# Merge-gate blocks placed between the column groups of an input projection, on one Trainium2 core

## The reference

```
xn = rmsnorm(h, norm_mix)
z = xn @ w_in
y_a = nsa_mixer(...) @ w_branch_nsa
y_b = dsa_mixer(...) @ w_branch_dsa
gate = sigmoid(g_merge)
h = h + (gate[..., :D] * y_a + gate[..., D:] * y_b) @ w_out
h = h + (silu(hn @ w_gate) * (hn @ w_up)) @ w_down
```

## Time and profile before

| | us |
|---|---|
| median of 3 runs | 1840.47 (1840.46 to 1841.13) |
| profiled execution, its own time | 1840.48 |
| span of the profiled execution | 1838.8 |
| TensorE busy in the span | 1707.3 (93%) |
| VectorE busy | 1208.7 (66%) |
| ScalarE busy | 701.4 (38%) |
| GpSimd busy | 567.1 (31%) |
| TensorE's share of the chain that ended last | 78% |

### The profile page before, as it was taken

One profiled execution on the slowest core, in us unless ns is written; L12 is line 12 of the kernel. 1 busy time (PEld: TensorE's weight loads), 2 busy tenths in 40 slices (PEclk: granted clock), 3 DMA queues, 4 the chain that ended last, 5 costly groups with the idle time before them and its releaser, 6 DMA issues.

```text
span 1838.8 us, 25573 instructions
## 1 busy us (share of the span) xinstructions
PE 1707.3 (93%) x9248; PEld 1467.2 (80%) x9248; DVE 1208.7 (66%) x2181; ACT 701.4 (38%) x1398; POOL 567.1 (31%) x396
## 2 busy tenths in 40 slices
PE   6789989999999999999999999899999999889994
PEld 5667778888898989889988877688888888668883
DVE  6689778999243545566646516667676676458976
ACT  5543433311274457655532114422322222234443
POOL 3303232322040012322212121544454445245451
PEclk9899989999999989999999999999999999989997
DMA  5103232532242001001015523122333222853432
GB/s 178 46 12 105 71 102 73 174 92 91 50 136 115 13 24 47 12 13 35 1 44 163 169 90 120 50 94 87 123 117 104 86 87 75 297 200 98 156 102 92
DMA packets 152590, 172.21 MB, mean 94 GB/s; under 512 B 18961, under 2 KB 102929, under 8 KB 152209
## 3 DMA queue, kind: packets, MB, share of 16 engines
q1 hardware_dynamic: 152464, 170.57, 28.9%
HBM read 121.00 MB, written 49.55 MB: 93 GB/s over the span
## 4 chain that ended last, share of the span: by engine, by line
PE 78%; DVE 10%; ACT 3%; DMA 3%; issue 3%; POOL 1%; SPq 1%; DVEq 0%; ACTq 0%; POOLq 0%
PE psA L1335 13%; PE psA L1336 13%; PE psA L1337 13%; PE psT L1517 9%; PE psT L1342 7%; PE psT L1336 5%; PE psT L1337 5%; PE psT L1335 5%; PE psA L1402 3%; PE psA L1401 3%; DMA act_raw<-scratch_act 1%; DVE rotated L1776 1%; DVE equal L1836 1%; POOL w_lo L377 1%; DVE above L1836 1%
## 5 line engine op out<-in xcount | busy, mean ns | idle before, releaser
L377 POOL TENSOR_TENSOR w_lo<-w_raw,w_hi 128x1024 fp32r<-128x1024 f32 (+2 forms) x52 | 119.9, 2314 | 243.3 <-ACT w_hi L372 243.3
L1188 ACT ACTIVATE p<-s,nmax 128x640 f32<-128x640 f32 (+7 forms) x192 | 143.9, 750 | 121.4 <-DVE nmax L1949 120.8
L995 POOL TENSOR_TENSOR w_lo<-w_sum,w_hi 128x1024 fp32r<-128x1024 f32 x44 | 115.5, 2626 | 129.4 <-ACT w_hi L1243 129.4
L1342 PE MATMUL psT<-ident,p 128*128 128x128 f32 x816 | 131.2, 282 | 19.2 <-DVE yTl_dsa L2008 4.7
L1018 POOL TENSOR_TENSOR w_lo<-act_raw,w_hi 128x512 fp32r<-128x512 f32 x77 | 104.9, 1366 | 137.8 <-ACT w_hi L1272 137.8
L2161 DVE TENSOR_TENSOR w_lo<-wd,w_hi 128x512 fp32r<-128x512 f32 x77 | 96.5, 1257 | 66.9 <-ACT w_hi L1279 66.6
L1335 PE MATMUL psA<-w_hi,xTh 128*128 128x512 f32 (+2 forms) x320 | 124.5, 389 | 13.6 <-POOL w_lo L377 9.5
L1336 PE MATMUL psA<-w_lo,xTh 128*128 128x512 f32 (+2 forms) x320 | 120.4, 376 | 0.0
L1337 PE MATMUL psA<-w_hi,xTl 128*128 128x512 f32 (+2 forms) x320 | 120.1, 375 | 0.0
L1342 PEld LDWEIGHTS psT<-ident,p 128*128 128x128 f32 x816 | 98.8, 154 | 26.4 <-ACT p L1188 7.0
L372 ACT CAST w_hi<-w_raw 128x1024 fp32r<-128x1024 f32 (+2 forms) x52 | 52.3, 1014 | 151.0 <-PE psA L1337 108.9
(11 more groups left out here) (351 smaller groups left out, 4949.1 us busy)
## 6 DMA issues: line engine op xcount, KB each, us to landing
act_raw<-scratch_act SPq DMA_DIRECT2D x77, 256.0 KB, 2.6
w_raw<-in_w_in_dram SPq DMA_DIRECT2D x28, 512.0 KB, 3.8
scratch_act<-act SPq DMA_DIRECT2D x33, 256.0 KB, 2.1
scratch_act<-act_sum SPq DMA_DIRECT2D x33, 256.0 KB, 2.1
scratch_gates<-gate_out SPq DMA_DIRECT2D x32, 256.0 KB, 3.1
gates<-scratch_gates SPq DMA_DIRECT2D x32, 256.0 KB, 4.1
wd<-in_w_down_dram SPq DMA_DIRECT2D x4, 1536.0 KB, 7.7
a<-in_w_gate_dram SPq DMA_DIRECT2D x22, 256.0 KB, 3.2
```

Source lines behind the costliest of these rows:

```text
L377: nc.gpsimd.tensor_tensor(self.lo[n % RING][:, 0:u], self.raw[n % RAW][:, 0:u], self.hi[n % RING][:, 0:u].bitcast(F32), ALU.subtract).then ...
L995: nc.gpsimd.tensor_tensor(lo2[n % RING][:], block_of(n)[:], hi2[n % RING][:].bitcast(F32), ALU.subtract)\
L1188: a_.activation(p_sb[v % PR][:, 0:n], s_sb[v % 2][:, 0:n], ACT.Exp, scale=-1.0, bias=nmax[:, BR[a], i, h:h + 1], accum_out=psum_p[:, BR[a] ...
L1342: mm = pe.transpose(bank[:, P * n:P * (n + 1)], src, ident[:])
```

## The change

The steps get one common list, `main`: after QB, CMP and WKV three gate blocks (six steps) each, after QA the other seven (14 steps). The list of weight pieces follows the same order. Slots, PSUM banks, loads, stores, spills, splits and turns go by positions in this list. A piece is due as before, at the step that frees its slot. ScalarE and GpSimd handle the first due piece ahead of their work on the step and the others behind it, which on ScalarE is behind `z_evac` but ahead of `block_hi` and `turned_out` of the steps before. VectorE does two passes of the bisection in each projection step and five in each gate step. Some hunks are left out: the release conditions of the ring slots and the bank number of an evacuation, rewritten for the new positions, and ScalarE's old gate loop.

```diff
--- before.py
+++ after.py
@@ -279,9 +279,18 @@
     def chunk_items(src, first, width):
         return [[(src[:, 2 * n:2 * n + 2, first:first + width], 0, 2, width)] for n in range(KT // 2)]

-    items1 = sum((chunk_items(w_in, *COLS[c]) for c in ORDER), [])
-    NCH = len(items1)
-    items1 += [[(w_in[:, :, o_gm + P * j:o_gm + P * (j + 1)], 0, KT, P)] for j in range(2 * KT)]
+    GATES_AFTER = {IDX: 0, QB: 3, CMP: 3, WKV: 3, QA: 7}
+    items1, main, chunk_at, gate_at = [], [], {}, []
+    for ch, c in enumerate(ORDER):
+        chunk_at[ch] = len(items1)
+        items1 += chunk_items(w_in, *COLS[c])
+        main += [("z", NT * ch + i) for i in range(NT)]
+        for _ in range(GATES_AFTER[c]):
+            j = len(gate_at)
+            gate_at.append(len(items1))
+            items1.append([(w_in[:, :, o_gm + P * j:o_gm + P * (j + 1)], 0, KT, P)])
+            main += [("g", 2 * j), ("g", 2 * j + 1)]
+    pos_of = {step: n for n, step in enumerate(main)}
     wa = A["w_branch_nsa"][0].rearrange("(k p) c -> p k c", p=P)
     wb = A["w_branch_dsa"][0].rearrange("(k p) c -> p k c", p=P)
     wo = A["w_out"][0].rearrange("(k p) c -> p k c", p=P)
@@ -332,7 +341,11 @@
     tg = {k: n for n, k in enumerate(tgroups)}

     Z_STEPS, G_STEPS = 8 * len(ORDER), 4 * KT
-    free1 = [8 * (n // 4) + 7 if n < NCH else Z_STEPS + 2 * (n - NCH) + 1 for n in range(len(items1))]
+    free1 = [0] * len(items1)
+    for ch, n in chunk_at.items():
+        free1[n:n + 4] = [pos_of["z", NT * ch + NT - 1]] * 4
+    for j, n in enumerate(gate_at):
+        free1[n] = pos_of["g", 2 * j + 1]
     M_STEPS, O_STEPS, F_STEPS = 2 * KT, 2 * NT, FT
     free2 = [2 * j + 1 for j in range(KT)] + [M_STEPS + 8 * (n // 4) + 7 for n in range(8)]

...
@@ -645,12 +657,6 @@
                 dst, src = kD["slc" if c == CMP else "win"][:, :, tok(i)], t[:, 0:4, :]
             sp.dma_start(dst, src.bitcast(F32)).then_inc(spilled[n % 2], 16)

-        for q in range(Z_STEPS + 3):
-            if q < Z_STEPS:
-                for n in w1.due(q, RAW + RING):
-                    w1.load(sp, n)
-            if q >= 3:
-                spill(q - 3)
         def load_q(k):
             set_, i = ("dsa", k) if k < NT else ("nsa", k - NT)
             if k >= 2:
@@ -665,15 +671,19 @@
             load_q(0)
             load_q(1)

-        for g in range(G_STEPS):
-            for n in w1.due(Z_STEPS + g, RAW + RING):
-                w1.load(sp, n)
-            if g == 4:
+        last_z = pos_of["z", Z_STEPS - 1]
+        for at_, (kind, n) in enumerate(main):
+            for item in w1.due(at_, RAW + RING):
+                w1.load(sp, item)
+            if kind == "g":
+                sp.wait_ge(g_out, n + 1)
+                sp.dma_start(gD[n // 2, :, HALF * (n % 2):HALF * (n % 2 + 1)], gst[n % 2][:])\
+                    .then_inc(g_stored[n % 2], 16)
+            if at_ >= 3 and main[at_ - 3][0] == "z":
+                spill(main[at_ - 3][1])
+            if at_ == last_z + 5:
                 sp.wait_ge(zt_ps, len(turned))
                 first_queries()
-            sp.wait_ge(g_out, g + 1)
-            sp.dma_start(gD[g // 2, :, HALF * (g % 2):HALF * (g % 2 + 1)], gst[g % 2][:])\
-                .then_inc(g_stored[g % 2], 16)


         sp.wait_ge(g_ps, G_STEPS)
@@ -897,13 +907,14 @@

         for n in range(RING):
             w1.split_lo(pool, n)
-        for q in range(Z_STEPS):
-            for n in w1.due(q, RING):
-                w1.split_lo(pool, n)
-            rope_cos(q)
-        for g in range(G_STEPS):
-            for n in w1.due(Z_STEPS + g, RING):
-                w1.split_lo(pool, n)
+        for at_, (kind, n) in enumerate(main):
+            due = w1.due(at_, RING)
+            for item in due[:1]:
+                w1.split_lo(pool, item)
+            if kind == "z":
+                rope_cos(n)
+            for item in due[1:]:
+                w1.split_lo(pool, item)

         pool.wait_ge(g_ps, G_STEPS)
         pool.wait_ge(pos_in, 16 * 4)
...
@@ -1097,16 +1108,26 @@
                     last = a_.copy(tq[s_ % 2][:, 4 * g:4 * g + 4, :], ps)
                 last.then_inc(zt_out, 1)

-        def stage2(first, stop):
-            for q in range(first, stop + 2):
-                if q < stop:
-                    for n in w1.due(q, RING):
-                        w1.split_hi(act, n)
-                    z_evac(q)
-                if first <= q - 1 < stop:
-                    block_hi(q - 1)
-                if first <= q - 2 < stop:
-                    turned_out(q - 2)
+        def gate_evac(g):
+
+            act.wait_ge(g_ps, g + 1)
+            if g >= 2:
+                act.wait_ge(g_stored[g % 2], 16 * (g // 2))
+            a_.activation(gst[g % 2][:], psA[:, pos_of["g", g] % 4, :], ACT.Sigmoid).then_inc(g_out, 1)
+
+        def stage2():
+            for at_ in range(NT, len(main)):
+                due = w1.due(at_, RING)
+                for n in due[:1]:
+                    w1.split_hi(act, n)
+                kind, n = main[at_]
+                (z_evac if kind == "z" else gate_evac)(n)
+                for n in due[1:]:
+                    w1.split_hi(act, n)
+                if main[at_ - 1][0] == "z" and at_ > NT:
+                    block_hi(main[at_ - 1][1])
+                if main[at_ - 2][0] == "z" and at_ > NT + 1:
+                    turned_out(main[at_ - 2][1])

         def id_relu(v):

@@ -1130,9 +1151,12 @@
                 for n in range(2, RING):
                     w1.split_hi(act, n)
             if 0 <= k - 1 < NT:
-                for n in w1.due(k - 1, RING):
+                due = w1.due(k - 1, RING)
+                for n in due[:1]:
                     w1.split_hi(act, n)
                 z_evac(k - 1)
+                for n in due[1:]:
+                    w1.split_hi(act, n)
             if 0 <= k - 2 < NT:
                 block_hi(k - 2)
             if 0 <= k - 3 < NT:
...
@@ -1358,21 +1375,26 @@
                 turn4(turn_bank(("x", i, g)), [xs[i % 2][:, P * k:P * (k + 1)] for k in range(4 * g, 4 * g + 4)])\
                     .then_inc(xt_ps, 1)

+        def bank_out(at_):
+
+            kind, n = main[at_]
+            return (z_out if kind == "z" else g_out), n + 1
+
         def z_step(q):
             c, i = zsteps[q]
             width = COLS[c][1]
-            if q >= 4:
-                pe.wait_ge(z_out, q - 3)
+            if pos_of["z", q] >= 4:
+                pe.wait_ge(*bank_out(pos_of["z", q] - 4))
             if q == NT:
                 pe.wait_ge(sc_done, len(iunits))
             if q < NT:
                 pe.wait_ge(xl_done, 2 * (q + 1))
             for a in range(KT // 2):
-                n = 4 * (q // NT) + a
+                n = chunk_at[q // NT] + a
                 if i == 0:
                     pe.wait_ge(w1.lo_done, n + 1)
                 hi, lo = w1.parts(n, 2)
-                mm = three(psA[:, q % 4, 0:width],
+                mm = three(psA[:, pos_of["z", q] % 4, 0:width],
                            [((xTh[:, 2 * a + k, tok(i)], xTl[:, 2 * a + k, tok(i)]), (hi[:, k, :], lo[:, k, :]))
                             for k in range(2)], a == 0, a == KT // 2 - 1)
                 if i == NT - 1 and a < KT // 2 - 1:
@@ -1388,12 +1410,20 @@
                     src = [kcvc[q % 2][:, P * b:P * (b + 1)] for b in range(2)]
                 turn4(turn_bank(("z", q, g)), src).then_inc(zt_ps, 1)

-        def stage2(first, stop):
-            for q in range(first, stop + 2):
-                if q < stop:
-                    z_step(q)
-                if first <= q - 2 < stop - 3:
-                    z_turn(q - 2)
+        def gate_step(g):
+            n, half = gate_at[g // 2], slice(HALF * (g % 2), HALF * (g % 2 + 1))
+            pe.wait_ge(w1.lo_done, n + 1)
+            pe.wait_ge(*bank_out(pos_of["g", g] - 4))
+            hi, lo = w1.parts(n, KT)
+            three(psA[:, pos_of["g", g] % 4, :], [((hi[:, k, :], lo[:, k, :]), (xTh[:, k, half], xTl[:, k, half]))
+                                                  for k in range(KT)]).then_inc(g_ps, 1)
+
+        def stage2():
+            for at_ in range(NT, len(main)):
+                kind, n = main[at_]
+                (z_step if kind == "z" else gate_step)(n)
+                if main[at_ - 2][0] == "z" and at_ > NT + 1:
+                    z_turn(main[at_ - 2][1])

         def scores(ps, q_, k_hi, k_lo, n):

@@ -1427,19 +1457,7 @@
                 id_unit(v)
         for v in range(EARLY, len(iunits)):
             id_unit(v)
-        stage2(NT, Z_STEPS)
-        for g in range(G_STEPS):
-            if g in (1, 2, 3):
-                z_turn(Z_STEPS - 4 + g)
-            n, half = NCH + g // 2, slice(HALF * (g % 2), HALF * (g % 2 + 1))
-            pe.wait_ge(w1.lo_done, n + 1)
-            if g < 4:
-                pe.wait_ge(z_out, Z_STEPS - 3 + g)
-            else:
-                pe.wait_ge(g_out, g - 3)
-            hi, lo = w1.parts(n, KT)
```

(50 more changed lines are left out.)

22 lines of the change are left out of this document (7 added, 15 removed).

## The result

Over 20 executions of each, the changed kernel takes **1846.31 us** (1843.22 to 1849.75) and the kernel before 1841.62 (1838.85 to 1845.89): ratio **1.0022, 95% interval 1.0015 to 1.0029**, slower by 4.1 us (2.8 to 5.3). The forecast was 1848.3 in a range of 1837 to 1855, with a chance of 0.70 for slower: the right side, with the time 2.0 us too high and the difference, +7.9 us, nearly twice the measured one. The profiled execution took 1847.43 us (span 1845.7).

What follows compares the result with a forecast made beforehand. TensorE was taken to set the time. Losses of 1.5 (slow start), 24.2 (entries), 9.6 (clock), 1.5 (exits) and 0.5 (VectorE's end) make 37.3 us against 29.4 before: +7.9 on 1840.48, so 1848.3 us, range 1837 to 1855.

Steps and rivals of the forecast that it cites:

- The mechanism: At group ends, block_hi queues on ScalarE behind three pieces, so block_lo is late; TensorE idles 6.5 us after QB's gate step.
- The entries: TensorE's stalls going from projection groups into gate blocks: 6.5 us at QB and QA, 4.3 CMP, 6.9 WKV; 24.2 together.
- The port: At the entries, GpSimd's running low half was taken to hold VectorE's block_lo; if not, 8.6 us less.
- rival A: block_lo isn't held by GpSimd's low half: 8.6 us less, 1839.7 us, no change; chance 0.13.
- The clock: TensorE at half clock after the four entry stalls, mean 2.4 us lost each: 9.6 us, bounds 7.4 and 12.
- Exits and tail: Gate blocks to the next group: 0.5 us each for three exits, 1.5 us; VectorE's end after QA: 0.5 us.
- so VectorE is through 75.6 us after it: After QA's released block_lo, VectorE's 32 passes (33.4 us) and selection (39.4 us), starting about 2.7 us behind it.
- the 353.1 needed: Time the five stretches from QB to the gates would need with turns counted where they stand: 353.1 us together.
- the slow start: Loss of about 1.5 us in the stretch that lies outside the change, counted among losses before and after.
- Passes and order at nothing: Single bisection passes on VectorE and the new order of splits: each costed at 0; order's bounds -1 and +1 us.
- IDX's end: First group's end under the new split order: evacuation earlier, block_hi a little later, scores start as now; 0 us.
- Rival B: Entries are hidden as intended, the fourth piece's cast ending by about 10.5: 24.5 us less, 1816 us; chance 0.09.

Runs made afterwards that it cites:

- experiment 1: Changed kernel, but after the first group ScalarE does block_hi and turned_out ahead of the second to fourth weight piece: 1823.85 us, ratio 0.9902.
- experiment 6: Changed kernel with block_hi and turned_out ahead of the second to fourth piece in all groups, the first too: 1820.64 us, ratio 0.9877.
- experiment 10: Kernel of experiment 6, with the fourth piece cast after the next gate step's evacuation and block_hi, and three passes per CMP step: 1822.63 us, ratio 0.9882.
- experiment 11: Kernel of experiment 6 unchanged, run again beside experiment 12 on one chip: 1823.15 us, ratio 0.9884 to the kernel before.
- experiment 12: Kernel of experiment 10 unchanged, run again beside experiment 11 on one chip: 1815.38 us, ratio 0.9846 to the kernel before.
- experiment 5: Kernel before, with single bisection passes alone: two per projection step behind IDX, the rest in the gate steps: 1840.24 us, ratio 0.9991.
- experiment 4: Kernel before, with the new order of splits alone (one piece ahead of the evacuation, others behind) on ScalarE and GpSimd: 1849.86 us, ratio 1.0037.
- experiment 7: Changed kernel, with bisection passes saved up until six are due and then made as a whole bit: 1854.79 us, ratio 1.0066.
- experiment 8: Changed kernel, with all due pieces split ahead of the evacuation on ScalarE and of rope_cos on GpSimd: 1849.42 us, ratio 1.0026.

## Why the prediction was right, and where its terms were off

**The mechanism** held as written, shown by experiment 1. Counted from the start of QB's last step (157.54), the forecast had the second low half from 7.8 to 10.2, the fourth cast from 14.0 to 15.0, block_hi done at 15.6, block_lo held to 17.5 and done at 18.2. Measured were 7.7 to 10.3, 14.2 to 15.2, 15.7, and TensorE going on at 18.2. The gate step ended at 12.0 and not 11.8.

**The size** is partly luck. The difference was forecast at +7.9 us and measured at +4.1 (2.8 to 5.3). The time itself came within 2.0 us because the forecast was added to one execution of the kernel before, 1840.48, where 20 have a median of 1841.62. In the profiled pair the stretch grew by 5.1 us where 7.4 were forecast.

**The entries** were 0.3, 0.6, 1.5 and 0.3 us shorter than forecast: 21.5 against 24.2. The largest error is WKV's: the first low half ended 4.6 us after the step's start and not 4.9, and was needed at 3.75 and not 3.5 (the cost there 0.94 and not 1.4); the wait for blocks behind it was 4.5 and not 5.5, which no single row explains.

**The port** was the doubtful term, taken from another instruction's rows. After has block_lo's own row, 2.34 us. The Trainium skill (SBUF — State Buffer, Who interferes with whom) has this rule, and the trace agrees: it picked the right one of two readings. Freed, the four waits lost 6.0 us; rival A priced it at 8.6. What a held block_lo loses is 2.34 less 0.68, 1.7 us, not the 2.4 of a whole low half; the forecast's own times (free to begin at 15.6, held to 17.5) already gave 1.9. The waits fell by 1.9, 0.8, 1.6 and 1.7.

**The clock.** TensorE from the four restarts (length, busy, granted clock, DMA share, GB/s):

```profile
175.76:182.50 6.74, 6.74 (x22) 0.57 0.82 272
264.55:271.30 6.75, 6.75 (x21) 0.57 0.54 160
334.70:338.10 3.40, 3.40 (x11) 0.57 0.80 212
425.24:432.00 6.76, 6.76 (x23) 0.59 0.84 268
```

Busy time times the missing share of the clock is 2.9 + 2.9 + 1.5 + 2.8 = 10.1 us, where 9.6 were forecast (bounds 7.4 and 12). Experiment 1's 9.2 us of busy time gained say the same from the other side.

**Exits and tail.** 1.5 us were charged for three exits, 0.5 for VectorE's end. In the changed kernel both were nothing: no exit shows a wait of 0.5 us, and VectorE's selection ended 4.3 us before it was needed. The reason given for the exits was sound all the same, only hidden under the stalls: with them gone, VectorE coming late out of its passes costs 1.0 to 1.5 us at the exit into WKV (experiments 1, 6, 10 to 12). The end of the selection:

```profile
496.91 0.70 DVE L1892 TENSOR_SCALAR score<-above 128x1024 f32<-128x1024 f32 x1
...
501.89 0.29 DVE L1972 CUSTOM_DVE_ANT_0 s<-psA,causal_bias 128x128 f32<-128x128 f32 x1 [4.28 <-PE psA L1432]
```

The step that failed is "so VectorE is through 75.6 us after it". After QA's last entry (TensorE on at 425.2) VectorE was through at 497.6, 72.4 us later: the passes ended 38.1 us after it where 36.1 were forecast, the selection (from 463.3) took 34.3 where the 39.4 of before were carried over. Both come from the low halves on GpSimd again. In the kernel before three instructions of the selection ran under one (at 431.65, 442.53 and 453.41) and lost 5.2 us by it; in the changed kernel the last low half is done at 460.7, and none did. The first and the third of them, before and after:

```profile
431.81 2.65 DVE L1862 SCALAR_TENSOR_TENSOR equal<-equal_so_far,need,equal 128x384 f32<-128x384 f32 x1
454.35 1.95 DVE L1859 TENSOR_SCALAR equal<-score,bit_try 128x896 f32<-128x896 f32 x1
...
465.57 0.62 DVE L1889 SCALAR_TENSOR_TENSOR equal<-equal_so_far,need,equal 128x384 f32<-128x384 f32 x1
484.14 0.68 DVE L1886 TENSOR_SCALAR equal<-score,bit_try 128x896 f32<-128x896 f32 x1
```

In the passes one decision, at 436.07, took 1.99 us in place of 0.17 under a low half, which is nearly all of their 2.0 us. TensorE needed 76.1 us to the first attention unit's scores and not 74.9. The bound was near all the same: in experiment 1, with a stretch 27 us shorter, VectorE was late by 1.1 us.

**The sum.** The forecast had 37.3 us lost, 0.5 of it behind the stretch, so 36.8 inside. Measured are 387.3 less the 353.1 needed, 34.2; before, the same difference is 29.0 against 29.4 read. Of the 34.2, idle rows hold 21.5, the clock 10.1 and the slow start 1.5; 1.1 us stand in no row. The error of -2.6 is thus -2.7 at the entries, -1.5 at the exits, +0.5 at the clock and +1.1 unassigned.

**Passes and order at nothing.** Costed at 0 each, and in sum that held only because they belong together. The passes alone give nothing that the whole time shows, the order alone costs 6.1 us in the old arrangement (experiments 5 and 4). In the new one whole bits would cost 8 us (experiment 7), and the old order 0.6 us of the stretch, which in the whole time can't be told (experiment 8: 1.0026 against 1.0022). IDX's end, forecast at 0: QB starts at 113.39 and not 113.62.

**Rival B**, the entries hidden as intended, was priced at 1816. Its condition, a quick landing, did not come true. Experiments 10 and 12 hide the entries in another way, by the order on ScalarE, and with one pass more in each CMP step: 1822.6 and 1815.4, on both sides of that price. The change could be worth 1.2 to 1.5%, and a wrong place in one queue turned that into a loss of 0.2%.

## What to carry to other kernels

When a refill is moved behind the work that it used to block, go on and ask what else stands behind it in the same queue: a cast that waits for a load belongs behind everything that the next step needs, not just behind the first such thing. A pause in a group's supply is not cured by one cheap step in between if the four transfers are chained through two buffers, because the chain is as long as before and now has one step for cover. And where TensorE's idleness is followed by half clock, judge a change by the stretch it touches, and by its idle and busy time apart: here the stretches of one kernel repeated within 1 us and the rest differed by 7 and 9, but experiment 5 shows that a stretch can hold such luck too.

## What the runs showed that I had not expected

**Tiny VectorE instructions are held too.** The threshold of a new bit works on 6 elements per partition and has one tensor input, yet it lasted as long as GpSimd's low half did beside it. From after, under the low half that runs from 160.39 to 163.10, then from a place with none:

```profile
160.76 2.36 DVE L1868 TENSOR_SCALAR bit_try<-bit_cur 128x6 int32<-128x6 int32 x1
...
337.76 0.16 DVE L1868 TENSOR_SCALAR bit_try<-bit_cur 128x6 int32<-128x6 int32 x1
```

The counting passes beside it, also with one tensor input but with an accumulator, keep their 0.61 to 1.27 us. The Trainium skill (SBUF — State Buffer, Who interferes with whom) names tensor_scalar, but not its form that writes out an accumulator, among the instructions that can take GpSimd's port if their operands allow it; these rows agree.

**A single short gap cost no clock, a long one did, and between them it went both ways.** TensorE in experiment 1 from the restarts behind gaps of 0.96 and 1.34 us (behind the third, 0.78, the clock was full too):

```profile
179.36:186.00 6.64, 6.64 (x34) 1.00 0.87 275
294.74:301.00 6.26, 6.19 (x48) 1.00 0.15 43
```

Gaps of 3.7 to 6.2 us in the changed kernel cost 1.5 to 2.9 us each on top of themselves. So shortening a long gap to a short one was worth more than the gap. But a gap of 3.09 us in the kernel before was followed by a granted clock of 0.54, and one of 3.03 us at the same place in experiment 5 by full clock (first row); and in the kernel before two short gaps close together, 1.03 and 0.65 us, were followed by half clock for most of the second row:

```profile
171.67:175.37 3.70, 2.96 (x12) 1.00 0.42 86
225.50:231.00 5.50, 4.25 (x20) 0.56 0.91 251
```

**The same code varies by 10 us.** With 7104 matmuls and 79.1 to 82.3 us of idle time, TensorE's busy time behind the stretch was 1262.27 to 1275.05 us in experiments 6 and 10 to 12. How the clock falls there was not settled; no experiment was aimed at it.
